# Down weights' low parts by adding transfers, squares taken from the bank, and one weight sum moved in a two-block transformer kernel

## What is computed

```python
D_MODEL = 1024
SEQ = 512
D_FF = 4 * D_MODEL

def sq_relu_mlp(h, w1, w2):
    return jnp.square(jax.nn.relu(h @ w1)) @ w2

    ...
        h = h + y
        h = h + sq_relu_mlp(rmsnorm(h, norm_mlp_g[i]), mlp_w1[i], mlp_w2[i])
```

## Time and profile before

| | us |
|---|---|
| median of 3 runs | 1768.1 (1767.79 to 1768.18) |
| the profiled execution, its own time | 1768.61 |
| its span, first to last instruction | 1766.8 |
| TensorE busy in the span | 1743.3 (99%) |
| VectorE, GpSimd, ScalarE busy | 1076.9, 867.1, 777.3 |

### The profile page before, as it was taken

One profiled execution on the slowest core, in us unless ns is written; L12 is line 12 of the kernel. 1 busy time (PEld: TensorE's weight loads), 2 busy tenths in 40 slices (PEclk: granted clock), 3 DMA queues, 4 the chain that ended last, 5 costly groups with the idle time before them and its releaser, 6 DMA issues.

```text
span 1766.8 us, 20727 instructions
## 1 busy us (share of the span) xinstructions
PE 1743.3 (99%) x8017; PEld 1430.8 (81%) x8017; DVE 1076.9 (61%) x1536; ACT 777.3 (44%) x1216; POOL 867.1 (49%) x375
## 2 busy tenths in 40 slices
PE   9999999999999999999999999999999999999998
PEld 7888778887888788888887887877877888888787
DVE  4794553766346589944465357477867960359743
ACT  5533445343234344554342234465545542455542
POOL 4343223577457669834576457544544544334221
PEclk9999999999999999999999999999999999999999
DMA  6232112345333423223344334433332333242111
GB/s 210 77 102 78 60 43 78 96 131 155 96 101 127 143 84 102 78 64 92 98 129 145 99 100 135 142 107 96 96 96 84 96 95 105 72 115 83 52 58 48
DMA packets 113154, 175.11 MB, mean 99 GB/s; under 512 B 12864, under 2 KB 39104, under 8 KB 113056
## 3 DMA queue, kind: packets, MB, share of 16 engines
q1 hardware_dynamic: 113056, 173.79, 32.4%
HBM read 170.09 MB, written 2.10 MB: 97 GB/s over the span
## 4 chain that ended last, share of the span: by engine, by line
PE 84%; DVE 8%; ACT 3%; DMA 2%; issue 1%; POOL 1%; SPq 0%; DVEq 0%; POOLq 0%; ACTq 0%
PE bank L712 25%; PE bank L714 25%; PE bank L713 25%; DMA w_raw<-in_mlp_w 2%; PE bank L1114 2%; PE bank L1058 1%; DVE w_raw L2150 1%; DVE w_raw L2149 1%; DVE residual L2175 1%; POOL w_lo L2818 1%; PE bank L916 1%; PE bank L798 1%; PE bank L898 1%; ACT w_hi L1366 1%; DVE w_raw L2157 1%
## 5 line engine op out<-in xcount | busy, mean ns | idle before, releaser
L2818 POOL TENSOR_TENSOR w_lo<-w_raw,w_hi 128x1024 fp32r<-128x1024 f32 (+1 forms) x310 | 786.5, 2546 | 853.0 <-ACT w_hi L1366 852.9
L1366 ACT ACTIVATE w_hi<-w_raw 128x1024 fp32r<-128x1024 f32 (+1 forms) x310 | 323.6, 1055 | 528.0 <-PE bank L714 443.1
L712 PE MATMUL bank<-x_hi,w_hi 128*128 128x512 f32 (+1 forms) x1264 | 501.9, 397 | 0.3 <-DVE x_lo L2603 0.3
L714 PE MATMUL bank<-x_hi,w_lo 128*128 128x512 f32 (+1 forms) x1264 | 492.5, 390 | 0.0
L713 PE MATMUL bank<-x_lo,w_hi 128*128 128x512 f32 (+1 forms) x1264 | 492.0, 389 | 0.0
L712 PEld LDWEIGHTS bank<-x_hi,w_hi 128*128 128x128 f32 (+1 forms) x1264 | 236.8, 187 | 53.5 <-issue 4.5
L713 PEld LDWEIGHTS bank<-x_lo,w_hi 128*128 128x128 f32 (+1 forms) x1264 | 236.9, 187 | 52.1 <-issue 3.8
L714 PEld LDWEIGHTS bank<-x_hi,w_lo 128*128 128x128 f32 (+1 forms) x1264 | 236.7, 187 | 50.9
L712 PE MATMUL bank<-w_hi,f_hi 128*128 128x512 f32 x480 | 187.9, 391 | 4.9 <-DVE residual L2175 3.7
L714 PE MATMUL bank<-w_hi,f_lo 128*128 128x512 f32 x480 | 186.9, 389 | 0.0
L713 PE MATMUL bank<-w_lo,f_hi 128*128 128x512 f32 x480 | 186.8, 389 | 0.0
(11 more groups left out here) (348 smaller groups left out, 2356.8 us busy)
## 6 DMA issues: line engine op xcount, KB each, us to landing
w_raw<-in_mlp_w SPq DMA_DIRECT2D x144, 512.0 KB, 3.8
w_raw<-in_even_w_in SPq DMA_DIRECT2D x48, 512.0 KB, 3.8
w_raw<-in_dsa_w_in SPq DMA_DIRECT2D x28, 512.0 KB, 3.7
w_raw<-in_odd_w_in SPq DMA_DIRECT2D x24, 512.0 KB, 3.7
w_raw<-in_conv_w_pw SPq DMA_DIRECT2D x32, 256.0 KB, 3.1
w_raw<-in_even_w_out SPq DMA_DIRECT2D x16, 512.0 KB, 3.8
w_raw<-in_dsa_w_out SPq DMA_DIRECT2D x8, 512.0 KB, 3.7
w_raw<-in_mlp_w SPq DMA_DIRECT2D x16, 256.0 KB, 3.1
```

Of the source, the lines that this page charges most:

```text
L712: e.matmul(o, sh, mh, start=first, stop=False)
L714: m = e.matmul(o, sl, mh, start=False, stop=last)
L1366: e.activation(hi, src, ACT.Copy).then_inc(*w_hi.up(u))
L2818: e.tensor_tensor(lo, src, hi.bitcast(F32), ALU.subtract).then_inc(*w_lo.up(u))
```

## The change

**Low parts by adding transfers.** Of each half's 22 down units, ten are marked `by_transfer`: the eight plain ones and the two of lower right blocks. For these ScalarE writes, behind the high part, a second rounding copy with scale -1 into the low slot, which then holds minus the high part. GpSimd, in place of its subtraction, issues a DMA from the raw slot into the low slot that adds to what stands there. Three semaphores in turn (`w_sent`) tell of the landings, and TensorE and SyncE wait for these (`low_of`). 270 units go on as before.

**Squares from the bank.** VectorE's square multiplies the bank by the ReLU of it, which stands in SBUF, where it multiplied the ReLU by itself. So TensorE gets the four banks back at the square and not at the ReLU.

**The second weight sum moved.** `second_sum(second[2])` now stands behind the additions that end with "y".

```diff
@@ weight_units, down
             if kind == "plain":
                 at += 2 * PAIRS
                 add(name, w2, [(n * 512, 512)], at, at + 2)
+                units[first].by_transfer = True
...
-                units[first].feeds = first + 2
+                units[first].feeds, units[first].by_transfer = first + 2, True
@@ signals
-        w_lo = signal("w_lo_split", every_unit)
+        w_lo = signal("w_lo_split", [u for u in every_unit if not units[u].by_transfer])
+        sent = [u for u in every_unit if units[u].by_transfer]
+        w_sent = [signal(f"w_lo_landed{i}", sent[i::3], 16) for i in range(3)]
+        def low_of(u):
+            return w_sent[sent.index(u) % 3].at(u) if units[u].by_transfer else w_lo.at(u)
@@ TensorE: two_tiles (and four like it)
-                w.wait_ge(*w_lo.at(u))
+                w.wait_ge(*low_of(u))
@@ TensorE: mlp
-                            free[BANKS[name][j]] = f_kept.at(layer, half, 4 * g + j)
+                            free[BANKS[name][j]] = f_squared.at(layer, half, 4 * g + j)
@@ ScalarE: split_to
-                    e.activation(hi, src, ACT.Copy).then_inc(*w_hi.up(u))
+                    m = e.activation(hi, src, ACT.Copy)
+                    if units[u].by_transfer:
+                        m = e.activation(lo, src, ACT.Copy, scale=-1.0)
+                    m.then_inc(*w_hi.up(u))
@@ VectorE: mlp
-                            e.tensor_tensor(f_raw(c), f_raw(c), f_raw(c), ALU.mult).then_inc(*f_squared.up(layer, half, c))
+                            e.tensor_tensor(f_raw(c), bank[BANKS[f"up{layer}{half}{g}"][j]][:, :], f_raw(c), ALU.mult).then_inc(*f_squared.up(layer, half, c))
...
                     second_sum(second[1])
-                    second_sum(second[2])
                     w.wait_ge(*used.at(first[9]))
...
                         add_product(layer, Y[i], i, 1, 1, down_added, layer, half, "y", i)
+                    second_sum(second[2])
@@ GpSimd: split_to
-                    e.tensor_tensor(lo, src, hi.bitcast(F32), ALU.subtract).then_inc(*w_lo.up(u))
+                    if units[u].by_transfer:
+                        e.dma_start(lo.bitcast(F32), src, accum_op=ALU.add).then_inc(*w_sent[sent.index(u) % 3].up(u))
+                    else:
+                        e.tensor_tensor(lo, src, hi.bitcast(F32), ALU.subtract).then_inc(*w_lo.up(u))
@@ SyncE: load_to
-                        w.wait_ge(*w_lo.at(u - RAW))
+                        w.wait_ge(*low_of(u - RAW))
```

More of the change, by code:

```diff
@@ L128, in __init__ @@
         self.name, self.index, self.per, self.cols, self.parts = name, index, per, cols, parts
-        self.added, self.feeds = None, None
+        self.added, self.feeds, self.by_transfer = None, None, False
 def weight_units(a):
@@ L1359, in split_to @@
                     u = split[0]
-                    src, hi, _ = ring(u)
+                    src, hi, lo = ring(u)
                     if units[u].added is not None:
```

## The result

| us | before | changed |
|---|---|---|
| median | 1768.05 (1767.45 to 1768.67, 6 runs) | **1780.74** (1779.17 to 1786.08, 6 runs) |
| the profiled execution, its own time | 1768.61 | 1780.11 |
| its span | 1766.8 | 1778.3 |

The changed kernel takes 1.0075 times the time of the one before (95% interval 1.0063 to 1.0088): 12.7 us slower. The forecast was 1763.8, its range ended at 1775.6; both missed.

A forecast was written before the change was run, and what follows sets the result against it. TensorE was taken to bound the kernel, busy 1743.3 of 1766.8 us. Border stalls -5.6 plus transfer stall 1.3 gave -4.3 us: 1764.3 for the profiled run, median 0.5 lower, 1763.8; range 1762.4 to 1775.6.

The forecast's parts named there:

- X: Time from GpSimd's reaching an adding transfer to its landing; taken as 5.2 us, with 7.6 as upper bound.
- (b): Forty low parts made by adding transfers instead of GpSimd subtractions; claimed to cost TensorE 1.3 us of stall.
- (a): Moving the second weight sum removes TensorE's 1.4 us stall at four borders between the two down products: gain 5.6 us.
- formula of the rivals: TensorE's stall: (X - 3.9) + 4(X - 5.3) + 4(X - 5.75) + 3(X - 6.0), each where positive.
- unit 58: Second plain unit of the first down product, layer 0, half 0; slack 3.9 us, claimed stall 1.3 us.
- 96-likes: Second plain unit of the first down product in the other three halves; slack 6.0 us, no stall claimed.
- 110-likes: Plain unit after the first one of the second down product, four times; slack 5.75 us, no stall claimed.
- Unit 61's 4.9: Slack in us of a plain unit, first down product, layer 0, half 0; claimed no cost beyond unit 58's.
- Rival 2: Slow transfer: above X = 6.2 each further 1 us costs 12 us; 1775.6 us at 6.6; chance 0.25.
- (c): Raw slots come free X minus 2.4 us later; the delayed raw loads were claimed covered, the second barely.
- (d): Squares taken from the bank, on VectorE; claimed cost 0 and gain 0.
- The others nothing: Claim that with X = 5.2 all transferred units except unit 58 cost TensorE no stall.

The follow-up runs named there:

- quiet loads: The changed kernel, with raw loads of the four units behind each transferred unit moving 16 of 128 partitions: 1763.87 us, ratio 0.998.
- The transfers alone: The changed kernel with the second weight sum back in its old place and the old squares, keeping all forty adding transfers: 1777.17 us, ratio 1.0051.
- eight of ten: The changed kernel with two of each half's ten transfers, those TensorE waited for, subtractions again, thirty-two transfers left: 1768.83 us, ratio 1.0003.
- twenty transfers: The changed kernel with five of each half's ten transfers kept, those ready 2.5 us or more before TensorE, the others subtractions again: 1762.59 us, ratio 0.9967.
- unmoved variant: The kernel with twenty transfers, but with the second weight sum back ahead of the additions: 1762.15 us, ratio 0.9971.

## Why the prediction was wrong

**The step that failed is X in (b)**: its stalls were put at 1.3 us and measured 14.7, with 1.4 more for the clock. Two things in it were wrong. Its size: one value, 5.2, was taken for forty transfers from rows of DMAs that say nothing of what ran beside them. Measured it is 4.5 to 4.6 where little else runs and 6.5 to 7.7 at the eight places where TensorE waits. The quiet loads show that the raw loads beside it are the cause. And its place in the range: I bounded the addition (7.6 above) but cut the range at 6.6, and named as doubts only an adder or an issue, never other traffic. The trace of before could have warned: behind the median of 3.8 us for the loads of 512 KB stand single ones that took up to 5.1.

**The parts were priced one by one, and they meet.** The prediction lets 105's low part end near 580.9, which frees a slot for a raw load, and starts 106's transfer near 581.2. So by its own times a load starts just ahead of the transfer, and it is (a) that puts it there. Seen from the border, both times came out within 0.4 us. The transfers alone, with the sum in its old place, lost 1.7 us at these four units instead of 6.8.

The prediction's estimate of 4.4 us from the Trainium skill ("DMA: Bandwidth & Descriptors", Anatomy of one DMA, with the second source read) agrees within 0.2 us with the 4.5 to 4.6 of a transfer with little beside it. The forecast by it was 1763.0, no nearer to the 1780.7 measured.

**The margins held where TensorE waited.** With the measured landings of the changed kernel the formula of the rivals gives for unit 58 6.8 - 3.9 = 2.9 (measured 2.82), for the 96-likes 7.5, 7.6 and 7.7 less 6.0, 1.5 to 1.7 (measured 1.63, 1.67, 1.78), for the first plain units of the second product 1.2 to 1.5 (measured 1.59 to 1.90). These last were 0.4 us worse than worked out: between ScalarE's second copy, ready at 587.51, and GpSimd's issue stand 0.6 us that I had left out.

```profile
586.47 1.04 ACT L1374 ACTIVATE w_lo<-w_raw 128x1024 fp32r<-128x1024 f32 x1
```

```profile
588.12 0.89 POOL L2828 DMA_DIRECT2D w_lo<-w_raw  x1 [0.77 <-ACT w_lo L1374]
```

The 110-likes, which the formula has next, never waited in the changed kernel, since their landings were 4.5 to 4.6. With eight of ten three of them did, and landing less stall gives 5.2 us there against 5.75, short by 0.5. Unit 61's 4.9 was no guide: it and its likes landed after 8.5 to 9.6, and TensorE never waited for them. GpSimd reached unit 61 at 384.31, 2.7 us sooner than worked out (386.98), and TensorE came later by unit 58's stall and the lower clock. Once 58 was a subtraction again, 61 did wait.

**Rival 2 is what happened**, a slow transfer, in its place and its sign (first plain units behind the border, TensorE waiting for a DMA). It was given 0.25, and at X = 6.6 priced at 13.1 us of stalls; there were 14.7. That the two sums are so near is partly luck: 3.4 of the 13.1 were priced at the 110-likes, which cost nothing. What it lacked is that X differs by place, and the 1.4 us of the lower clock behind the first stall.

**(a)** was right at three borders. In layer 0, half 0, with the sum moved alone, the stall went to X2, 1.15 us. The times of (a) had shown this, had X2 been worked out for that border too: the eight additions from 403.5 on, the moved sum and three more end near 412.2, and the bank is wanted at 408.23 + 2.72 = 410.95. (a) worked it out for the second border alone. In the changed kernel even this is covered. With twenty transfers the move has no share that can be shown, as the unmoved variant is as fast, and with forty it seems to cost. I had priced the subtraction's interference as part of (a) and not seen that (b) takes that same subtraction away, by turning the lower right block's into a transfer. (The row of 568.93 to 574.45 that it reads as one subtraction is two, the lower right block's and the next unit's; the second sum met both.)

**(c)** was right in its result, that TensorE waits for no raw load in the MLPs, but not in its term: it took 3.8 us for a load, and loads beside a transfer took up to 9.9. VectorE's waits for raw loads in the MLPs rose from 60.3 to 75.7 us, off TensorE's path. **(d)** was right: no wait, no gain to be measured.

**"The others nothing"** fell with X. That some transfers are free and a few carry the loss was in part to be had from the margins listed in (b), had they been read as a choice of places and not as one sum: the twenty that proved free all had 7 us or more there.

## What to carry to other kernels

When an engine's step is handed to a DMA, compare its landing, measured beside the loads that are in flight at that very place, with the slack of every single place; a median or a value of an idle machine decides nothing. Hand over only the places whose slack is larger, and expect that a removed stall may uncover the next ones behind it. Ask of every other edit whether it moves a load next to the transfer. When two edits attack the same wait (here a moved sum, and a subtraction turned into a transfer), run each alone before you keep both.

## What the runs showed of the hardware

- **An adding transfer holds the DMA engines twice as long** as a copy of the same bytes and packets: 45.5 against 21.9 engine-us for 512 KB. With little beside it, it lands 4.5 us after GpSimd reaches it, the copy 2.9, and GpSimd's issue took 0.88 us against 0.58.
- **Landing times grow with the traffic beside them**: the same adding transfer took 4.5 to 9.6 us, the copy 2.9 to 7.2; with an eighth of the loads' bytes the adding transfer took 4.5 to 6.5, with a median of 4.6. The raw loads suffer too: the longest landing of a load in the MLPs rose from 5.1 to 9.9 us, with a median of 3.8 in both kernels.
- **TensorE's clock after an idle stretch**: after 2.66 us without work the granted clock was 0.66 over the next 5 us, and after 3.6 us 0.50; in another kernel it was 1.00 after 2.61 us at the same place. What decides between these the runs don't show.
- **VectorE and GpSimd took turns**: an operation of a weight sum took 0.68 us and 2.88 us when a subtraction ran beside it; with a transfer in place of the subtraction, 0.68 again. The Trainium skill ("SBUF — State Buffer", SBUF: two separate sides) says that a VectorE operation with two operands in SBUF and a GpSimd one that reads SBUF exclude each other for the whole instruction. By that rule the trace agrees.
